# A recurrence in rounds: score products of the next tile in the last phases of a round, and sample states on quarters

## What is computed (the reference, cut)

```python
kk = k * k_k; kk = kk / max(sqrt(sum(kk * kk)), 1e-12)
k = k * (1.0 + (a - 1.0) * k_a)
def step(S, inp):                       # per head, S is 64 x 64
    r_t, w_t, k_t, v_t, a_t, b_t = inp  # a_t = -kk, b_t = kk * a
    sa = einsum('bhij,bhj->bhi', S, a_t)
    S = S * w_t[:, :, None, :] + sa[..., None] * b_t[:, :, None, :] + v_t[..., None] * k_t[:, :, None, :]
    y = einsum('bhij,bhj->bhi', S, r_t)
yn = (y - mean) * rsqrt(var + GN_EPS) * lnx_g + lnx_b
yn = yn + sum(r * k * r_k) * v
out = (yn * g) @ w_o
```

## Time and profile before

| | us |
|---|---|
| median of 3 runs | 2278.16 |
| lowest, highest | 2270.88, 2286.08 |
| profiled execution, its own time | 2273.13 |
| profiled execution, span | 2271.3 |
| busy: TensorE, VectorE, ScalarE, GpSimd | 2063.1, 1333.9, 746.4, 198.4 |

### The profile page before, as it was taken

The page is one execution under the profiler, slowest core; times in us unless marked ns, Lnnn a source line. Parts: engine busy times, 40 slices in busy tenths (PEclk is TensorE's granted clock), DMA queues, the critical chain, the costliest instruction groups (busy, mean ns, idle before and its releaser), DMA issues.

```text
span 2271.3 us, 37176 instructions
## 1 busy us (share of the span) xinstructions
PE 2063.1 (91%) x15388; PEld 1915.9 (84%) x15388; DVE 1333.9 (59%) x2123; ACT 746.4 (33%) x1290; POOL 198.4 (9%) x199
## 2 busy tenths in 40 slices
PE   2989988888888978989999998999899989999996
PEld 2988876766667758989999998999568989999996
DVE  7675566567666534787436644425574787526754
ACT  3443443233333321422212213322683522112222
POOL 3000223211322100000000000000330000000000
PEclk9999978778788868999999999999999999999998
DMA  2211000000000022122222222241652122222221
GB/s 106 91 58 61 11 1 13 12 3 13 13 11 3 12 75 98 56 75 70 70 86 73 68 70 86 75 158 41 240 182 94 56 75 70 70 84 75 68 70 58
DMA packets 30325, 150.69 MB, mean 66 GB/s; under 512 B 4784, under 2 KB 7600, under 8 KB 17872
## 3 DMA queue, kind: packets, MB, share of 16 engines
q1 hardware_dynamic: 30160, 148.32, 18.9%
HBM read 137.84 MB, written 10.47 MB: 65 GB/s over the span
## 4 chain that ended last, share of the span: by engine, by line
PE 60%; DVE 6%; ACT 2%; issue 1%; DMA 0%; DVEq 0%; POOL 0%; ACTq 0%; SPq 0%; POOLq 0%
PE ps L600 16%; PE ps L602 16%; PE ps L601 16%; PE ps L1925 1%; PE ps L666 1%; PE ps L664 1%; PE ps L665 1%; PE ps L1945 1%; PE ps L1914 1%; PE ps L1324 1%; DVE w_lo L595 1%; DVE split_f L811 1%; DVE gate_e L931 1%; PE ps L1939 1%; PE ps L1909 1%
## 5 line engine op out<-in xcount | busy, mean ns | idle before, releaser
L600 PE MATMUL ps<-x_hi,w_hi 128*128 128x320 f32 x2208 | 694.0, 314 | 67.3 <-DVE x_lo L718 41.3
L601 PE MATMUL ps<-x_lo,w_hi 128*128 128x320 f32 x2208 | 690.5, 313 | 0.0
L602 PE MATMUL ps<-x_hi,w_lo 128*128 128x320 f32 x2208 | 690.0, 313 | 0.0
L600 PEld LDWEIGHTS ps<-x_hi,w_hi 128*128 128x128 f32 x2208 | 422.2, 191 | 72.3 <-issue 46.9
L595 DVE TENSOR_TENSOR w_lo<-raw,w_hi 128x2048 fp32r<-128x2048 f32 (+2 forms) x110 | 229.7, 2089 | 412.7 <-ACT w_hi L589 412.7
L601 PEld LDWEIGHTS ps<-x_lo,w_hi 128*128 128x128 f32 x2208 | 422.4, 191 | 0.2
L602 PEld LDWEIGHTS ps<-x_hi,w_lo 128*128 128x128 f32 x2208 | 421.9, 191 | 0.0
L589 ACT ACTIVATE w_hi<-raw 128x2048 fp32r<-128x2048 f32 (+2 forms) x110 | 192.0, 1745 | 420.9 <-PE ps L602 420.9
L602 PE MATMUL ps<-hid_hi,w_lo 128*128 128x320 f32 x704 | 217.5, 309 | 0.0
L600 PE MATMUL ps<-hid_hi,w_hi 128*128 128x320 f32 x704 | 217.5, 309 | 0.0
L601 PE MATMUL ps<-hid_lo,w_hi 128*128 128x320 f32 x704 | 217.5, 309 | 0.0
(11 more groups left out here) (263 smaller groups left out, 3116.1 us busy)
## 6 DMA issues: line engine op xcount, KB each, us to landing
raw<-in_w_gate SPq DMA_DIRECT2D x22, 1024.0 KB, 4.8
raw<-in_w_up SPq DMA_DIRECT2D x22, 1024.0 KB, 4.9
raw<-in_w_down SPq DMA_DIRECT2D x16, 768.0 KB, 4.2
raw<-in_w_down SPq DMA_DIRECT2D x16, 640.0 KB, 3.9
raw<-in_w_kv SPq DMA_DIRECT2D x8, 1024.0 KB, 4.8
past_k<-in_past_k SPq DMA_DIRECT2D x8, 1024.0 KB, 7.1
past_v<-in_past_v SPq DMA_DIRECT2D x8, 1024.0 KB, 4.9
raw<-in_w_r SPq DMA_DIRECT2D x4, 1024.0 KB, 7.2
```

The source lines that it names most:

```text
L600: pe.matmul(out, w, x, start=start, stop=False)
L601: pe.matmul(out, w, xl, start=False, stop=False)
L602: return pe.matmul(out, wl, x, start=False, stop=stop)
```

## The change

The part ahead of phase 0 is dissolved. The five score steps of tile i+1 (not i) are made in phases 15 to 19 of round i, one a phase, on banks 4 and 5; those of tile 0 stand before round 0. The logits come at phase 0, the transposes of `bk` at phases 1 and 2, the bonus sums and the norms at phase 2, each behind the merge of its phase. The output of tile i-2 comes at phases 15, 17 and 18. The steps of the preparation move: the reciprocals of `gate_a` to phases 2 to 5, those of `sig_w` to 6 to 9, the scan to 10, the sums to 11, the exponentials to 12, the products of `bk` and `ra` to 13 and 14; GpSimd makes the query factor in two pieces. The centring, the variance, the scaling and the bonus are at phases 0, 2, 4 and 15.

For the samples, `s_ar` (the head-masked copy) is gone: `s_from` takes rows of one head at a time and has both heads' rows in its result; `spread` holds both heads with four streams on each half of the rows, so that `s_state` is eight products (K = 64, M = 64, 256 columns) on the four quarters of the array, at phase 14, in two banks. SyncE loads `low_g2` behind the stores of the states.

```diff
-    s_ar = ring0("s_ar", [2, 2, NS * TS])
-    s_from = ring0("s_from", [2, 2, NS * TS], rows=HD)
+    s_from = ring0("s_from", [2, NS * TS])
...
-    for k, step, hh in ((4, "s_from", 0), (6, "s_pre", 0), (7, "s_u", 0), (9, "s_out", 0),
-                        (10, "s_state", 0), (13, "s_state", 1)):
+    for k, step, hh in ((4, "s_from", 0), (6, "s_pre", 0), (7, "s_u", 0), (9, "s_out", 0), (14, "s_state", 0)):
...
+    FIRST_GRAM = SLOTS - NT
+    OUTPUT_AT = {15: "y_t", 17: "sv_t", 18: "zg"}
+
+    def gram_plan(f, u):
+
+        for hh in range(2):
+            take(("gram", f, hh, u), 4 + hh)
...
+            if tile_of(i + 1) and k == 0:
+                take(("zw", i + 1), 4, 2)
+                take(("za", i + 1), 6, 2)
+            if tile_of(i) and k == 1:
+                take(("bk_tok", i, 0), 4)
+                take(("bk_tok", i, 1), 5)
+            if tile_of(i) and k == 2:
+                take(("bk_tok", i, 2), 4)
+                take(("bonus", i), 5)
+            if tile_of(i + 1) and k == 2:
+                take(("ss", i + 1), 6, 2)
...
+                    elif step == "s_state":
+                        for g, bank in enumerate((4, 7)):
+                            take(("s_state", i - 1, g), bank)
...
+            if tile_of(i + 1) and k >= FIRST_GRAM:
+                gram_plan(i + 1, k - FIRST_GRAM)
+            if tile_of(i - 2) and k in OUTPUT_AT:
+                take((OUTPUT_AT[k], i - 2), 6, 2)
...
     def pe_rec(pe, i):
-        if tile_of(i + 1):
-            pe_logits(pe, i + 1)
-        if tile_of(i):
-            pe_grams(pe, i, 0, 3)
-        if tile_of(i + 1):
-            pe_norms(pe, i + 1)
-        if tile_of(i):
-            pe_grams(pe, i, 3, NT)
-            pe_by_token(pe, i)
         for k in range(SLOTS):
             if tile_of(i):
                 pe_merge(pe, i, k)
-            if tile_of(i - 2) and k < 2:
-                pe_output(pe, i - 2, k)
+            if tile_of(i + 1) and k == 0:
+                pe_logits(pe, i + 1)
+            if tile_of(i) and k in (1, 2):
+                pe_by_token(pe, i, k)
+            if tile_of(i + 1) and k == 2:
+                pe_norms(pe, i + 1)
             if tile_of(i - 1):
                 pe_states(pe, i - 1, k)
+            if tile_of(i + 1) and k >= FIRST_GRAM:
+                pe_grams(pe, i + 1, k - FIRST_GRAM)
+            if tile_of(i - 2) and k in OUTPUT_AT:
+                pe_output(pe, i - 2, OUTPUT_AT[k])
...
+    def pe_grams(pe, f, u):
+
+        if u == 0:
+            for made in ("a_made", "b_made", "k_decayed"):
                 pe.wait_ge(S(made), f + 1)
...
+        pe.wait_ge(S("r_made"), 2 * f + (1 if u < NPT - 1 else 2))
+        at = slice(u * P, (u + 1) * P)
+        banks = [claim(pe, ("gram", f, hh, u)) for hh in range(2)]
...
+        for j in ((0, 1) if k == 1 else (2,)):
...
+        if k == 2:
+            pe.wait_ge(S("rk_made"), f + 1)
...
-                    mm = pe.matmul(ps[0:HD, bank, s * 4 * TS:(s + 1) * 4 * TS].rearrange("p (c t) -> p c t", c=4), state_s[:, s, :],
-                                   s_ar[:, :, :, s * TS:(s + 1) * TS].rearrange("p h q t -> p (h q) t"), start=True, stop=True)
+                    for hh in range(2):
+                        rows = slice(hh * HD, (hh + 1) * HD)
+                        mm = pe.matmul(ps[rows, bank, s * 2 * TS:(s + 1) * 2 * TS].rearrange("p (q t) -> p q t", q=2), state_s[rows, s, :],
+                                       ra[rows, b, :, TP + s * TS:TP + (s + 1) * TS], start=True, stop=True)
                 fill(mm, ("s_from", f))
...
+                pe.matmul(ps[:, bank, 0:P], s_from[:, A_OF, :], ident, start=True, stop=False)
                 for hh in range(2):
-                    out = ps[:, bank, hh * HD:(hh + 1) * HD]
-                    pe.matmul(out, s_from[:, hh, A_OF, :], ident[0:HD, 0:HD], start=True, stop=False)
-                    mm = pe.matmul(out, score(f, hh, SAMPLE, "ka"), v_of(f, SAMPLE, hh), start=False, stop=True)
+                    mm = pe.matmul(ps[:, bank, hh * HD:(hh + 1) * HD], score(f, hh, SAMPLE, "ka"), v_of(f, SAMPLE, hh), start=False, stop=hh == 1)
...
-                bank = claim(pe, ("s_state", f)) if n == 0 else place[("s_state", f)][0]
-                pe.wait_ge(S("spread_made"), 2 * f + n + 1)
-                pe.wait_ge(S("v_spread_made"), 2 * f + n + 1)
-                out = ps[n * HD:(n + 1) * HD, bank, :].rearrange("p (s i) -> p s i", s=NS)
-                pe.matmul(out, bk_tok[:, b, SAMPLE, 0, n * HD:(n + 1) * HD], spread[:, 0, :, :], start=True, stop=False)
-                mm = pe.matmul(out, bk_tok[:, b, SAMPLE, 1, n * HD:(n + 1) * HD], spread[:, 1, :, :], start=False, stop=True)
-                if n:
-                    fill(mm, ("s_state", f))
...
+                banks = [claim(pe, ("s_state", f, g)) for g in range(2)]
+                pe.wait_ge(S("spread_made"), f + 1)
+                pe.wait_ge(S("v_spread_made"), f + 1)
+                for q in range(2):
+                    for g, bank in enumerate(banks):
+                        rows = slice(g * HD, (g + 1) * HD)
+                        for hh in range(2):
+                            out = ps[hh * HD:(hh + 1) * HD, bank, 0:HALF_STATES].rearrange("p (s i) -> p s i", s=NS // 2)
+                            mm = pe.matmul(out, bk_tok[rows, b, SAMPLE, q, hh * HD:(hh + 1) * HD], spread[rows, q, hh, :, :],
+                                           start=q == 0, stop=q == 1)
+                        if q:
+                            fill(mm, ("s_state", f, g))
+
+    def pe_output(pe, f, step):
...
+            if tile_of(i + 1) and k == 0:
+                act_sigmoids(act, i + 1)
+            if tile_of(i - 2) and k == 1:
+                act.wait_ge(S("y_centred"), i - 1)
+                act.activation(r_t[:, i - 2, :], k_t[:, i - 2, :], ACT.Square).then_inc(S("y_squared"), 1)
+            if tile_of(i) and k in (2, 3):
+                act_by_token(act, i, k)
+            if k == 3:
+                act_roots(act, i + 1, i - 2, chain)
             if tile_of(i - 1):
                 act_states(act, i - 1, k)
...
+            if i == NF and k == SLOTS - 1:
+                act_x_hi(act, "o", NF - 2, r_t[:, NF - 2, :], emptied_at("zg", NF - 2))
+            if tile_of(i + 1) and k == SLOTS - 1:
+                act_seeds(act, i + 1)
...
     def act_prepare(act, f, k, chain):
-        if k == 7:
+        if k == 12:
 
...
-        elif k == 8:
...
-            for hh in range(2):
-                ins = pool.tensor_scalar(s_ar[:, hh, :, :], ra[:, f % 2, :, TP:T], tab("head")[:, hh:hh + 1], 1.0, MUL, MUL)
-            ins.then_inc(S("s_ar_made"), 1)
...
+            if tile_of(i - 1) and k == 6:
+
+                f = i - 1
+                if f:
+                    filled(pool, ("s_state", f - 1, 1))
+                if f >= 2:
+                    filled(pool, ("sv_t", f - 2))
+                pool.tensor_tensor(spread[:, 1, :, :, :],
+                                   v_tok[:, SAMPLE, f * P:(f + 1) * P].rearrange("p (h i) -> p h i", h=2).unsqueeze(2)
+                                   .broadcast_to([P, 2, NS // 2, HD]),
+                                   stream_of_row(), MUL).then_inc(S("v_spread_made"), 1)
+            if tile_of(i + 1):
...
+        elif k == 13:
...
-        elif k == 14:
-
-            if f >= 2:
-                filled(pool, ("y", f - 2, NPT - 1))
-                pool.wait_ge(S("s_ar_made"), f - 1)
-            pool.tensor_tensor(ra[:, f % 2, R_OF, :], r_t[:, f, :], c_mid[:, :], MUL).then_inc(S("r_made"), 1)
+            for n, at in ((NPT - 2, slice(0, TP - P)), (NPT - 1, slice(TP - P, T))):
+                if f >= 2:
+                    filled(pool, ("y", f - 2, n))
+                pool.tensor_tensor(ra[:, f % 2, R_OF, at], r_t[:, f, at], c_mid[:, at], MUL).then_inc(S("r_made"), 1)
...
         for k in range(SLOTS):
             if tile_of(i) and PHASES[k][0] != "inv":
                 dve_merge(dve, i, k)
-            if tile_of(i - 2) and k < 2:
-                dve_output(dve, i - 2, k)
+            if tile_of(i + 1) and k == 0:
+                dve_keys(dve, i + 1)
+            if tile_of(i + 1) and k == 1:
+                dve_one_plus(dve, i + 1, chain)
+            if tile_of(i + 1) and k == 2:
+                dve_norms(dve, i + 1)
+            if tile_of(i - 2):
+                if k == 0:
+                    dve_centre(dve, i - 2, chain)
+                elif k == 2:
+                    dve_variance(dve, i - 2)
+                elif k == 4:
+                    dve_normed(dve, i - 2)
+                elif k == 15:
+                    dve_bonus(dve, i - 2)
             if tile_of(i - 1):
                 dve_states(dve, i - 1, k, chain)
             if tile_of(i + 1):
                 dve_prepare(dve, i + 1, k, chain)
+            if tile_of(i + 1) and k >= FIRST_GRAM:
+                dve_grams(dve, i + 1, k - FIRST_GRAM)
+            if tile_of(i - 2) and k >= 16:
```

(72 more changed lines are left out.)

229 lines of the change are left out of this document (76 added, 153 removed).

## The result

The changed kernel takes 2318.28 us (median of 4 runs, 2316.57 to 2320.95) against 2281.88 us before in the same comparison (4 runs, 2270.88 to 2286.08): a ratio of 1.0171, 95% interval 1.0142 to 1.0200 (ratios are given as recorded; the quotient of the two medians is 1.0160). It is slower, by 1.4 to 2.0%. The forecast was 2237 in a range of 2185 to 2300; the time lies within 1 us of rival (b), "the clock stays down", 2319, which had a chance of 0.18.

The account below looks back on a forecast made before the run. TensorE was seen busy nine tenths of the span, but at a lowered clock in the recurrence. Round 0 +9, six full rounds -36, round 7 -6, round 8 -9 and ends +1 gave -41 from 2278.2: 2237 us, range 2185 to 2300.

Parts of the forecast that it names:

- rival (b): Recurrence: once fallen in phases 2 to 5, the clock stays down; 48 us a round at half clock, 2319 us; chance 0.18.
- the sum: Full recurrence round: phases 0 to 5, 6 to 14 and 15 to 19 total 56.5 us at full clock against 60.2.
- the quarters: Sample states' product: 16 instructions, four at a time, take 0.9 us, a gain of 2.8; s_pre and s_out save some 0.6.
- I take L = 22 us instead of 27: Full rounds: time at half clock falls from 27 to 22 us, making a round 67.5 us, 6 less, 36 over six.
- the second fall loses its cause: Phases 15 to 19: the clock's second fall loses its cause, since scores and outputs fill the holes there.
- probably stays: The clock's first fall in a round, 24 us at half clock in round 3 before, probably stays after the change.
- The other rounds: Outside the six full rounds: round 0 +9 us, round 7 -6, round 8 -9, last output and first projection +1.
- rival (a): Recurrence: holes fall away and the clock stays up; 5 us at half clock, round 59 us, about 2186 us; chance 0.16.
- a tenth or two: Sample states on quarters: a drain of the array at a mode change would add this much; left out of the sum.
- Within 2 us: Sign of being right: phase 0's merge product follows the last one of the round before within 2 us.
- Gap-free in phases 15 to 19: Sign of being right: TensorE has no gaps in phases 15 to 19, where score and output steps were moved.
- (c): Moved work does not fit behind the phases, as waiting steps hold the next merge; round 72 us, about 2265; chance 0.20.

Follow-up runs that it names:

- e5: The changed kernel with norms, centring, square and variance reordered in phases 0 to 3 to close TensorE's hole; 2295.76 us (ratio to before 0.9996).
- e3: The changed kernel plus 48 idle TensorE products of 512 columns, one in each packing phase; 2249.24 us (ratio to before 0.9868).
- e4: The kernel before plus 48 idle TensorE products of 512 columns, one in each packing phase; 2275.08 us (ratio to before 0.9965).
- e2: The kernel before, in its old order, with only the sample states' product put on quarters at phase 14; 2291.63 us (ratio to before 1.0036).
- e12: The kernel before with sample states on quarters, plus 48 idle TensorE products of 256 columns; 2251.31 us (ratio to before 0.9864).
- e10: The kernel before with sample states on quarters, plus 48 idle TensorE products of 512 columns; 2207.11 us (ratio to before 0.9697).
- e1: The changed kernel in its new order, with the sample states' product back on two halves of 512 columns; 2319.27 us (ratio to before 1.0169).
- e11: The changed kernel's new order with sample states on halves, plus 48 idle TensorE products of 512 columns; 2278.82 us (ratio to before 0.9987).
- e6: The changed kernel with waits of phases 0 to 3 mended, plus 48 idle TensorE products of 512 columns; 2239.43 us (ratio to before 0.9821).
- e8: The changed kernel plus 96 idle TensorE products of 512 columns, two in each packing phase; 2282.14 us (ratio to before 1.0000).

## Why the prediction was wrong

**The content was right.** By its own terms the sum held -3.7 us of content for each of six rounds, and +9 - 6 - 9 + 1 for the rest: -27 us. Measured: -29, good to some 5 us. As F comes out too low where L is high (e5), this number alone would be weak; e3 against e4, at nearly the same L, gives -26 by the medians. Round 3's stretches come to 6.6 + 21.9 x 0.53 = 18.2, 27.4 x 0.85 = 23.3 and 17.3 x 0.84 = 14.5 us at full clock, where 19.5, 23 and 14 were forecast. The six rounds are 54.6 us on average against 56.5. Inside this the parts were off both ways: the quarters, taken at 3.4 us a tile, brought 34 to 38 us over eight tiles, 4.3 to 4.8 each, while the new order brought 7 on halves and cost 9 on quarters (444 to 453), so that the sum came out closer than its terms.

**The step that failed is "I take L = 22 us instead of 27".** The 27 came from round 5's content of 60; over the six rounds before, at a mean clock of 0.80, L is 30. After, it is 41.8 us in the six rounds: 75.5 us each are 54.6 of content plus 20.9. The difference to the forecast is (41.8 - 22) / 2 = 9.9 us a round, 59 over six; less content gives 11 back. The text had noted that the wide state products preceded the rise of the clock in four of six rounds and were to go, and then put no price on it. e2, e12 and e10 bear the link out: with quarters in their place L goes up by 106 us, and wide products that compute nothing bring it down again, the more the wider they are. It is not the whole: e1 keeps the wide state products and still has an L of 388. The other half of the reason, "the second fall loses its cause", was right in its place (phases 15 to 19 of round 6 run at 0.99, those of round 3 at 0.84, against 0.70 in the earlier trace rows), and was outweighed by the first fall. That one, which "probably stays", did so in round 3 (21.9 us at 0.53, against 24 before; L of the whole round is 34 both times) and grew in others: rounds 4 and 6 have L 51 and 55, where the kernel before has 35 and 32:

```profile
527.70:604.10 76.40, 65.31 (x536) 52.82 (x534) 49.13 (x104) 26.66 (x58) 17.04 (x14) 0.77 0.03 10
...
673.10:745.80 72.70, 63.13 (x539) 52.52 (x537) 49.63 (x104) 26.78 (x58) 18.91 (x15) 0.78 0.03 10
```

**The other rounds.** The start was forecast at +9 and took +11 (68.7 against 57.3, up to tile 1's first merge: 260.31 to 317.56). Rounds 7 and 8 were forecast at -15, with no term for the clock, and took +30 in the stretch from tile 7's first merge to the end. This is the second step that failed, 45 us, nearly as much as the first one's 48. Again it is not content, which fell there from 90 to 82 us; L rose from 48 to 124. Round 7 of the kernel before, at a clock of 0.91, had been the model for rival (a); the same round, tile 7's, now runs at a mean of 0.56 from that merge on (779.73 to 853.33).

**Quarters.** 16 instructions in 1.99 us at half clock, 1.09 in e10 at full clock: four at a time, as forecast. Its row, beside the idle product and the packed transposes that follow it:

```profile
465.92 1.08 PE L1291 MATMUL ps<-table 128*128 128x512 f32 x2
466.84 0.72 PE L1294 MATMUL ps<-table,inv_f 128*128 128x128 f32 x4
...
474.73 0.39 PE L1374 MATMUL ps<-v_tok,gram 128*128 128x64 f32 x2
474.96 0.39 PE L1375 MATMUL ps<-u_tok,gram 128*128 128x64 f32 x2
475.27 1.09 PE L1420 MATMUL ps<-spread,bk_tok 64*64 64x256 f32 x16
```

The two wide products took 3.7 us at full clock. The Trainium skill, TensorEngine Tiling (Array Packing), Tiling Modes, says that a change of mode drains the array. What these rows allow for it is small: the last pair of 128 by 128 products takes 0.31 us to the first quarter (474.96 to 475.27), the pair before it, with one of its own form behind it, 0.23 (474.73 to 474.96). That is some 0.1 us, the lower end of the prediction's "a tenth or two".

**What was to be seen.** "Within 2 us" became 1.49 us of wait behind the last score. "Gap-free in phases 15 to 19": not quite, 0.52 + 0.95 + 1.49 us and one of 0.20 at the fourth score step, 3.2 us together, against 0.9 by hand. The sign for (b), "a granted clock near 0.5 from phase 5 to 15 of each round", came in part: the clock falls earlier still, from phase 2, and stays at half in round 6, but phases 6 to 14 of round 3 ran at 0.85.

**The rivals.** (b) had the mechanism; its L of 48 a round was 6 too high and its content 2 too high, 30 us over six rounds, and for rounds 7 and 8 it had about -10 where +30 came, so that its 2319 is right by luck: errors of 30 and 40 us cancel. (c) is real but small: mending its waits gives some 16 us of content (e5's profiled run). (a) was priced as though a filled hole brought the clock back. The Trainium skill, TensorE: Matmul & The Clock Gate, HAM oscillation, leads there with its gaps between bursts. In e5's profiled run the largest gap of a round was closed and the clock stayed at 0.68, and in round 6 of the changed kernel it stayed at half for 32 us with hardly a gap, so gaps are not the whole cause here; e5's faster runs leave open how large a part they have.

**Still open:** why the new order lowers the clock even where the wide state products are kept (e1: L 388 against 256). Closing the hole does not cure it reliably (e5) and idle products do (e11: 199, near e4's 184), which fits a stretch of phases with too little streamed in it, but no run moved a single step of the order to show which.

## What to carry to other kernels

When the clock moves within a stage, split the stage into length times clock and time at half clock, and forecast both: here some 25 to 30 us of savings came with 170 us more at half clock. Half of that time is more likely too much than too little for its cost: in e5's runs it cost a third. Narrow fp32 products that fill TensorE's rows did not bring its clock back here, so a change that removes wide products, even wasteful ones, needs a term for the clock; one trial with a few idle wide products in the waits tells at once whether the clock is the loss and what a good change is hiding (e2 to e10: 85 us). Put in as few as hold it, since each costs most of its time. And test the parts of a change apart at a held clock: the dissolved head, which looked like the better half, was worth nothing by itself there (2275 to 2279) and cost 42 us beside the quarters.

## What was not expected of the hardware

TensorE ran at half clock for 32 us in which its rows covered 93% of the time (29.88 of 32.00 us, 730.00 to 762.00). Forty-eight idle products of 512 columns made the same program 3.0% faster (2318.28 to 2249.24 in the changed kernel) or 3.7% (2291.63 to 2207.11 with the old order and quarters), of 256 columns 1.8% (2291.63 to 2251.31), of 8 columns nothing. One program's runs differed by 51 us, and the clock with them (e5: 2265.79 at a mean of 0.917, 2316.44 at 0.886); 152 us more at half clock cost a third of that in time. The runs of e3, e4, e6 and e10, with one idle product of 512 columns a phase, stayed within 2 to 6 us (e11's within 10, e8's, with two, within 15).
